# The gated layers' up products by Winograd's form of Strassen: seven half-size products for eight

## The reference

```
def swiglu_ffn(h, w1, w3, w2):
    return (jax.nn.silu(h @ w1) * (h @ w3)) @ w2

for layer in range(DEPTH_2):
    hn = rmsnorm(h, norm_mix_g[layer])
    ...
    h = h + mix
    h = h + swiglu_ffn(rmsnorm(h, norm_ffn_g[layer]), ffn_w1[layer], ffn_w3[layer], ffn_w2[layer])
return rmsnorm(h, final_g)
```

## Time and profile before

| | |
|---|---|
| median of 3 runs | 1737.45 us (1736.9 to 1738.46) |
| profiled execution: span | 1736.2 us |
| median over that span | 1.25 us more |
| TensorE, busy | 1723.5 us (99%), 8050 matmuls |
| VectorE, ScalarE, GpSimd, busy | 817.1, 688.5, 740.6 us |
| gated layer 0, from group 0's last quarter on | 738.28 to 1097.32 us |
| gated layer 1, the same | 1381.47 to 1724.2 us |

### The profile page before, as it was taken

The page is one execution under the profiler, slowest core; times in us unless marked ns, Lnnn a source line. Parts: engine busy times, 40 slices in busy tenths (PEclk is TensorE's granted clock), DMA queues, the critical chain, the costliest instruction groups (busy, mean ns, idle before and its releaser), DMA issues.

```text
span 1736.2 us, 23746 instructions
## 1 busy us (share of the span) xinstructions
PE 1723.5 (99%) x8050; PEld 1418.5 (82%) x8050; DVE 817.1 (47%) x1457; ACT 688.5 (40%) x1041; POOL 740.6 (43%) x329
## 2 busy tenths in 40 slices
PE   9999999999999999999999999999999999999998
PEld 7877778888888788888888888888888888888887
DVE  5655565333333678532332335566665523323425
ACT  5566553222222434632322224565655432322324
POOL 3232325444446297444354353442424353443441
PEclk9999999999999999999999999999999999999999
DMA  7442223322222133233233233231212332332231
GB/s 199 113 102 79 73 65 117 98 97 97 97 97 97 61 116 107 84 101 97 85 109 97 85 109 97 74 97 48 87 58 74 97 110 85 98 107 85 97 96 49
DMA packets 153686, 162.25 MB, mean 93 GB/s; under 512 B 10628, under 2 KB 114680, under 8 KB 153632
## 3 DMA queue, kind: packets, MB, share of 16 engines
q1 hardware_dynamic: 149167, 158.66, 29.7%
q10 hardware_dynamic: 4464, 2.89, 0.5%
HBM read 157.84 MB, written 3.67 MB: 93 GB/s over the span
## 4 chain that ended last, share of the span: by engine, by line
PE 95%; DVE 2%; ACT 1%; issue 0%; DMA 0%; SPq 0%; DVEq 0%; ACTq 0%
PE ps L1295 83%; PE ps L1316 2%; PE ps L1751 1%; PE ps L1643 1%; PE ps L1324 1%; PE ps L1514 1%; PE ps L1533 1%; DVE ps L2279 1%; PE ps L1426 0%; PE ps L1420 0%; PE ps L1784 0%; PE ps L1497 0%; PE ps L1430 0%; PE ps L1742 0%; PE ps L1498 0%
## 5 line engine op out<-in xcount | busy, mean ns | idle before, releaser
L640 POOL TENSOR_TENSOR wlo<-raw,whi 128x1024 fp32r<-128x1024 f32 x228 | 550.2, 2425 | 765.9 <-ACT whi L730 750.9
L1295 PE MATMUL ps<-h_hi,wlo 128*128 128x512 f32 x1376 | 546.1, 397 | 0.8 <-DVE gv L2045 0.3
L1295 PE MATMUL ps<-h_hi,whi 128*128 128x512 f32 x1376 | 536.6, 390 | 0.0
L1295 PE MATMUL ps<-h_lo,whi 128*128 128x512 f32 x1376 | 536.2, 390 | 0.0
L730 ACT ACTIVATE whi<-raw 128x1024 fp32r<-128x1024 f32 x282 | 292.7, 1055 | 503.7 <-PE ps L1295 495.1
L1295 PE MATMUL ps<-m_hi,wlo 128*128 128x512 f32 x800 | 314.5, 393 | 0.0
L1295 PE MATMUL ps<-m_hi,whi 128*128 128x512 f32 x800 | 311.5, 389 | 0.0
L1295 PE MATMUL ps<-m_lo,whi 128*128 128x512 f32 x800 | 311.4, 389 | 0.0
L1295 PEld LDWEIGHTS ps<-h_hi,whi 128*128 128x128 f32 x1376 | 258.3, 188 | 55.1
L1295 PEld LDWEIGHTS ps<-h_hi,wlo 128*128 128x128 f32 x1376 | 258.5, 188 | 54.2 <-issue 1.6
L1295 PEld LDWEIGHTS ps<-h_lo,whi 128*128 128x128 f32 x1376 | 258.6, 188 | 51.1 <-issue 0.5
(11 more groups left out here) (311 smaller groups left out, 1621.1 us busy)
## 6 DMA issues: line engine op xcount, KB each, us to landing
raw<-in_ffn_w SPq DMA_DIRECT2D x264, 256.0 KB, 2.8
raw<-in_w_ff SPq DMA_DIRECT2D x128, 256.0 KB, 2.8
raw<-in_hg_w_in SPq DMA_DIRECT2D x64, 256.0 KB, 3.1
raw<-in_w_in SPq DMA_DIRECT2D x40, 256.0 KB, 5.2
raw<-in_cp_w_in SPq DMA_DIRECT2D x24, 256.0 KB, 2.9
raw<-in_w_out SPq DMA_DIRECT2D x16, 256.0 KB, 2.9
raw<-in_cp_w_out SPq DMA_DIRECT2D x16, 256.0 KB, 2.9
raw<-in_hg_w_out SPq DMA_DIRECT2D x16, 256.0 KB, 2.9
```

The source lines that it names most:

```text
L640: pool.tensor_tensor(wlo[:, u % RING, :, :], raw[:, u % RING, :, :], whi[:, u % RING, :, :].bitcast(F32), ALU.subtract).then_inc(unit_lo, 1)
L1295: mm = pe.matmul(ps[:, b, :], wt[:, s, a, m * P:(m + 1) * P], xt[:, kts[a], :], start=starts and a == 0 and i == 0, stop=last)
```

## The change

From group 2 on, each block of an up product (w1 or w3, 256 hidden columns, all 1024 of the width, 512 tokens) is taken as a 2 x 2 product of halves (halves of the hidden columns, of the width and of the tokens) and made by seven products of 128 hidden columns, 512 of the width and 256 tokens, in place of eight. There are 18 such blocks per layer, numbered j = 0 to 17, even ones w1, odd ones w3.

- TensorE, `products(j, ...)`: per block 7 products of 4 k-tiles x 3 parts, 256 columns each. The results `y1, u2, u3, p5, c11, c12, c21` go to banks 0 to 3 in turn, so that a bank is used again three products after it is full. Down parts of two groups are put together in one `down_pair` of 96 matmuls, after every fourth block. Groups 0 and 1 are done as before. Order per layer: up 0, up 1, block 0, down pair, three turns of (blocks of four, down pair), five blocks, down pair, down of the last group.
- VectorE: four sums of quarter blocks of the weights (`weight_sum`), the low parts of forms 0, 1, 2, 3 and 5 (`low`), and the sums of the products (`add_u2` to `add_c21`), which before were two drains per block; the tokens now come normed, so `rs` is not applied there.
- GpSimd: low parts of forms 4 and 6 (`plain_low`) and of all down units, 512 columns at a time (`down_low`).
- ScalarE: the high part of each of the seven forms (`high`), a copy of `y1`, and `silu` in parts.
- Tokens: VectorE makes the normed tokens (eight tiles, `normed_tokens`), four sums of token quarters, and the low parts of seven token forms (`token_lo`, 4 x 256 columns each); ScalarE their high parts. For this the norm's sum is moved: `norm_sum` stands behind 36 of group 0's matmuls instead of 72, `sum_top` ahead of the units' splits, and three of group 0's and 1's splits behind `inv_rms`.
- Weight forms lie in 12 slots of 512 columns, eight of them the old ring. The weight transfers keep their bytes; a unit of a block has four k-tiles of 256 columns, in two transfers.

The diff, cut to its core:

```diff
+FORMS = 7
+TAGS = ("y1", "u2", "u3", "p5", "c11", "c12", "c21")
+SUM_OF = {1: 2, 2: 3, 3: 1, 5: 4}
+LOW_ON_VECTOR = (0, 1, 2, 3, 5)
+LOW_ON_GPSIMD = (4, 6)
+HALF = SEQ // 2
+SLOTS = 12
+PAIRS_IN_LOOP = 3
...
+def block_banks(j):
+    at = [(b - j) % 4 for b in (0, 1, 2, 3, 0, 1, 2)]
+    return [((tag, j), b) for tag, b in zip(TAGS, at)]
...
 # GpSimd
+                def plain_low(j, i=None):
+                    for f in LOW_ON_GPSIMD:
+                        n = block_slot(j) + f
+                        s = form_slot(layer, n)
+                        pool.wait_ge(form_hi, at(i, N_TURN, SLOTS_USED * layer + n + 1))
...
+                        pool.tensor_tensor(in_tiles(lo_slot(s)), form_source(layer, j, f),
+                                           in_tiles(hi_slot(s)).bitcast(F32), ALU.subtract).then_inc(plain_lo, 1)
...
 # ScalarE
-                def norm():
-                    sum_top(5 + 2 * layer)
-                    inv_rms(5 + 2 * layer)
-
-                up(0, 0, 0, 0, 0, norm, layer)
...
+                sum_top(5 + 2 * layer)
                 if layer == 0:
+                    split(first, 0)
+                inv_rms(5 + 2 * layer)
+                for j in range(1, 4):
+                    split(first, j)
+                for f in range(4):
+                    token_hi(f)
...
 # TensorE
+                def products(j, slots_before, i=None):
+                    for f in range(FORMS):
+                        s = form_slot(layer, block_slot(j) + f)
+                        b = part_bank(layer, j, TAGS[f])
+                        x_hi, x_lo = rounded_tokens(f)
...
+                        pe.wait_ge(drained[b], part_nth(layer, j, i, TAGS[f]) - 1)
+                        for k in range(4):
+                            for p, (wt, xt) in enumerate(((lo_slot(s), x_hi), (hi_slot(s), x_lo), (hi_slot(s), x_hi))):
+                                begins, ends = k == 0 and p == 0, k == 3 and p == 2
+                                mm = pe.matmul(ps[:, b, 0:HALF], wt[:, k * P:(k + 1) * P], xt[:, k, :],
+                                               start=begins and TAGS[f] != "c11",
+                                               stop=ends, skip_group_check=TAGS[f] == "c11")
...
-                group(first, 0, stage, up_tags, 0, 0, (0, 2, 1, 3), 0, n, norm_after(5 + 2 * layer, 2))
-                with pe.Fori(0, GLU_GROUPS // 2) as i:
-                    up(4, i * 2 + 1, i, 12)
-                    down(8, i * 2, 0, i, 12)
-                    up(10, i * 2 + 2, i, 12)
-                    down(14, i * 2 + 1, 1, i, 12)
-                down(6 * GLU_GROUPS - 2, GLU_GROUPS - 1, 0, 0, 0)
+                group(first, 0, stage, up_tags, 0, 0, (0, 2, 1, 3), 0, n, None, lambda: norm_sum(5 + 2 * layer), 1)
+                group(first, 4, stage, up_tags, 0, 0, (0, 2, 1, 3), 1)
+                products(0, 0)
+                down_pair(FORMS, 0, 0, lambda kt: pe.wait_ge(ghid_lo, 4 * layer + kt + 1))
+                with pe.Fori(0, PAIRS_IN_LOOP) as i:
+                    products(1, 2, i)
+                    for j in range(2, 5):
+                        products(j, 1, i)
+                    down_pair(N_LOOP + 4 * FORMS, 8, i + 1, parts_made(0, i), i)
+                products(TAIL, 2)
+                for j in range(TAIL + 1, TAIL + 5):
+                    products(j, 1)
...
 # VectorE
+                def normed_tokens():
+                    for k in range(KT):
+                        dve.scalar_tensor_tensor(out=n1[:, k, :] if k < 4 else ps[:, k, :], in0=xT[:, k, :],
+                                                 scalar=col("norm_ffn_g_2", KT * layer + k), in1=rs[:, :],
+                                                 op0=ALU.mult, op1=ALU.mult).then_inc(tokens_made, 1)
+                    token_step(t3[:, :, :], n2[:, :, HALF:], n1[:, :, HALF:], ALU.subtract, 8)
+                    token_step(t2[:, :, :], t3[:, :, :], n1[:, :, 0:HALF], ALU.add, 9)
+                    token_step(n1[:, :, HALF:], n1[:, :, HALF:], n1[:, :, 0:HALF], ALU.subtract, 10)
...
+                def during_up(x, y, gate_before=None, i=None):
+                    if gate_before is not None:
+                        add_c21(gate_before, i)
+                    weight_sum(y, 1, i)
+                    weight_sum(y, 2, i)
+                    low(y, 0, i)
+                    weight_sum(y, 3, i)
+                    low(y, 1, i)
+                    add_u2(x, i)
+                    low(y, 2, i)
+                    weight_sum(y, 4, i)
+                    add_u3(x, i)
+                    low(y, 3, i)
+                    add_p5(x, i)
+                    low(y, 5, i)
+                    gated_c11(x, i)
+                    add_c12(x, i)
+                    gated_c12(x, i)
...
+                dve.wait_ge(rs_ready, 6 + 2 * layer)
+                normed_tokens()
+                up_drain(0)
```

More of the change, by code:

```diff
@@ L127, in before, with glu_banks @@
         return self.nth(name, tag, turn) - 1
+def glu_banks(b, layer, up, down):
+    b.stage(f"glu{layer}", up, 2)
+    b.stage(f"glu{layer}tokens", [(("n", k), 4 + k) for k in range(4)])
+    b.stage(f"glu{layer}first", block_banks(0))
+    b.stage(f"glu{layer}loop", [x for j in range(1, 5) for x in block_banks(j)], PAIRS_IN_LOOP)
+    b.stage(f"glu{layer}tail", [x for j in range(TAIL, TAIL + 5) for x in block_banks(j)])
+    b.stage(f"glu{layer}down", down, PAIRS_IN_LOOP + 3)
 def bank_plan():
@@ L1684, in glu @@
                 first, stage = U_GLU[layer], f"glu{layer}"
-                done = 2 * GLU_GROUPS * layer
-                def up(j0, g, turn, per):
-                    group(first, j0, stage, up_tags, turn, per, (0, 2, 1, 3), g)
-                def down(j0, g, par, turn, per):
-                    for h in range(2):
-                        def tile(a):
-                            pe.wait_ge(ghid_lo, g * 2 + (done + a + 1))
-                        unit(first, j0 + h, m_hi, m_lo, (2 * par, 2 * par + 1), stage,
-                             [("d", h, m) for m in range(4)], True, True, turn, per, use=g, wait_tile=tile)
@@ new lines, in down_pair @@
+                def down_pair(n0, d0, turn, tile, i=None):
+                    for q in range(4):
+                        h, p = q // 2, q % 2
+                        s = [form_slot(layer, n0 + 2 * q + a) for a in range(2)]
+                        pe.wait_ge(down_lo, at(i, 8, DOWN_SLOTS * layer + d0 + 2 * q + 2))
+                        begun = False
+                        for a, m in [(a, m) for m in range(4) for a in range(2)] if p else [(a, m) for a in range(2) for m in range(4)]:
+                            kt = 2 * p + a
+                            if m == 0:
+                                tile(kt)
+                            if p == 0 and a == 0:
+                                pe.wait_ge(drained[4 + m], before(stage + "down", ("d", h, m), turn))
+                            for r, (wt, xt) in enumerate(((lo_slot(s[a]), m_hi), (hi_slot(s[a]), m_lo), (hi_slot(s[a]), m_hi))):
+                                last = p == 1 and a == 1 and r == 2
+                                mm = pe.matmul(ps[:, 4 + m, :], wt[:, m * P:(m + 1) * P], xt[:, kt, :],
+                                               start=kt == 0 and r == 0, stop=last)
+                                if not begun:
+                                    mm.then_inc(form_used, 2 if q else 1)
+                                    begun = True
+                                if last:
+                                    mm.then_inc(filled[4 + m], 1)
@@ L1705, in _ @@
+                for h in range(2):
+                    unit(first, LATER_UNITS + 4 + h, m_hi, m_lo, (4, 5), stage + "down", downs[h], True, True,
+                         use=PAIRS_IN_LOOP + 2, wait_tile=lambda a: made(4 + a))
             glu(0, 3)
@@ new lines, in glu @@
+                low(0, 5)
+                up_drain(1)
+                token_lo(4)
+                up_hidden(1)
+                add_u2(0)
+                token_lo(5)
+                for k in range(4):
+                    dve.sem_inc(filled[4 + k], 1)
+                add_u3(0)
+                token_lo(6)
+                up_lo(1)
+                add_p5(0)
+                dve.wait_ge(tokens_lo, FORMS * layer + 6)
+                for k in range(4):
+                    dve.sem_inc(drained[4 + k], 1)
```

610 lines of the change are left out of this document (541 added, 69 removed).

## The result

The changed kernel takes 1726.8 us (median of 4 runs, 1725.71 to 1727.73) against 1737.5 for the kernel before: ratio 0.9938, with a 95% interval of 0.9924 to 0.9952. It is faster by 10.7 us where 31 were forecast. 1726.8 lies inside the range of 1686 to 1738 and outside the forecast's own range of 1695 to 1718.

What follows compares the result with a forecast made beforehand. The prediction took TensorE, busy 99% of the span, as the bound. 1736.2 - 49.0 (short matmuls) + 12.7 (head) + 5 (VectorE in blocks) = 1704.9 us of span, median 1706; range 1686 to 1738.

Steps and rivals of the forecast that it cites:

- the forecast's own range: Whole kernel: the range of the forecast's main case, 1695 to 1718 us, given a chance of 0.50.
- The pitch of the short matmul: TensorE's blocks: a 256-column matmul takes 113.3 ns, half of 226.7, giving -49.0 us in two layers.
- the rival with the fixed excess: TensorE's blocks: 13.3 ns excess per instruction, so 120.0 ns a short matmul, kernel 1722 us; chance 0.24.
- the floor by the loads: TensorE's blocks: overlapping weight loads come no closer than 111.5 ns, giving -54 us in two layers.
- the 427 ns at 1.2 GHz: TensorE at half clock: the 512-column matmul showed no excess, taken as pointing to a stream-rate limit rather than a fixed cost.
- My own sign of being wrong: TensorE's blocks: the forecast is wrong if the pitch is over 120 ns or gaps in the blocks exceed 1 us each.
- the turn of 62.1: Loop of four blocks and a down pair: 62.1 us if the pitch is 0.120, against 59.9 us forecast.
- the estimate from the Trainium skill: TensorE's blocks: 262 cycles for 256 columns, 109.2 ns, which would give -61.5 us in two layers; not adopted.
- the rival of the exposed load: TensorE's blocks: each product waits for its whole 188 ns weight load, kernel slower at 1927 us; chance 0.05.
- VectorE in the blocks, +5: Blocks: VectorE, partly held up by GpSimd's low parts, runs late and costs 2.5 us per layer, +5 in two.
- The head, +12.7: Start of each gated layer: late first drains (4 and 4), layer 1's late norm (2.7) and slowed clock (2), +12.7 us.
- The shared inputs as a rival: Blocks: every GpSimd low part stops VectorE, prepared blocks last 10.9 and 12.1 us, kernel slower at 1749; chance 0.11.

Runs made afterwards that it cites:

- Experiment 1: A program of its own, not an edit of the kernel: streams of 96 matmuls of various widths; float32r took 120.0 ns at 256 columns, 226.7 at 512.
- experiment 7: Changed kernel with all seven low parts of a block on VectorE, none on GpSimd: 1726.8 us, ratio 0.9933.
- experiments 8 and 10: Changed kernel with block products over 192 of 256 token columns: 1715.7 us; the second also cuts GpSimd's two low parts per block to 16 columns: 1699.7 us.
- Experiment 2: Changed kernel with GpSimd's low parts of units 2 to 7 in the gated layers' head cut to 8 of 512 columns: 1712.7 us, ratio 0.9858.
- experiment 3: Changed kernel with the inverse norm also written to PSUM, where the eight normed tokens read it: 1716.8 us, ratio 0.9880.

## Why the prediction was wrong, by its steps

**The pitch of the short matmul: the step that failed.** "I take 113.3": measured 120.0 ns, the rival with the fixed excess, to which I gave 0.24. 3024 x 6.67 = 20.2 us, which is nearly all of the 20.8 by which the time was missed. I weighed the half of a known pitch and the floor by the loads against the excess, and let the 427 ns at 1.2 GHz decide. The numbers for both were there; 427 ns at half clock, with no excess, did not tell what a shorter stream does at full clock. Why there is an excess, and why none at half clock, no run here shows. My own sign of being wrong, "over 120", stood just beyond the rival's 120.0 and so could not tell the two apart; the turn of 62.1 could. Experiment 1 gives 120.0 with all other engines idle. The 109.2 ns that the estimate from the Trainium skill gave (TensorE: Matmul & The Clock Gate, Back-to-back issue gap) comes out in the same program with bfloat16 operands, 109.4 and 215.8; for float32r the measurement decides, 120.0.

**The floor by the loads: right.** 111.5 ns at 192 and 128 columns. The load was not exposed. In the last sentence on the rival of the exposed load I misread a row: the matmuls of 111.7 ns have 128 columns, whose stream is 53.3 ns and not 106.7. What it argues stands without it, since a load recorded at 188 ns doesn't fit into 111.7 unless it overlaps.

**VectorE in the blocks, +5: 0 was measured** (no wait in the loop; experiment 7 the same). The mechanism was right, as experiments 8 and 10 show: at 111.5 ns the locked low parts cost 1.8 us a turn and 16 us in all. At 120 they lie within the block's 10.08. The charge and the pitch were not independent: the fast pitch would have run into VectorE, and the rival with the fixed excess had rightly taken the charge back to +1.

**The head, +12.7: 17.5 was measured, and 0.6 elsewhere.** The kernel gained 10.7 where the pitch alone gives 28.8. Of the 18.1 the waits show 7.4 for the first drain (forecast 4 and 4), 2.6 for layer 1's norm (2.4 and 0.2 for its two matmuls; 2.7 forecast), 1.4 before block 0 and 1.0 in the first down pair (neither forecast), and the clock took 1.4 and 1.7 (2 in all forecast). Layer 0's 4.6 is to the tenth what I worked out before I rounded it down, and its terms came out too: 12.3 us for the eight tokens where the prediction had 12.5. Layer 1's came to 2.8, since the slow clock behind the norm had already made TensorE 1.7 us late there. Counted from start to start of the matmuls, against 226.7 and 120.0 ns, layer 0 loses 7.3 us and layer 1 10.2; half of the 2 us beyond the list is that each of the six gaps is 0.16 longer from start to start than the idle time shown, and the rest lies in single steps. The 0.6 us left lie outside the gated layers. Experiment 2 gets 14 of the 18 back by taking GpSimd's inputs away, experiment 3 gets 10 with the whole computation kept.

**The shared inputs as a rival** were placed wrong: they decide in the head, not in the blocks. The rule of the Trainium skill (SBUF — State Buffer, SBUF: two separate sides), by which GpSimd holds up a VectorE operation with two SBUF inputs, agrees with 3.42 and 3.10 us for operations of 1.22, and with the tokens of experiment 3, which have one and run at full pace.

**The terms add up**: the pitch was taken 20.2 us too short, the head and the rest 5.4 too short, the blocks 5 too long: 20.6 of the 20.8.

## What to carry to other kernels

This matmul, float32r with 128 stationary columns, kept its excess over the stream when it was cut from 512 columns to 256: price a shorter form with the excess in full, and run the one instruction alone when a whole change hangs on it. Where VectorE and GpSimd both read two SBUF inputs, handing work to GpSimd took almost nothing off VectorE here; one operand in PSUM freed both. Before moving an instruction forward, look at what is queued behind its wait, and on which other engine somebody waits for that; and a gap that has its cause upstream only changes its place when the instruction is moved.

## What the hardware showed that I had not expected

- Float32r with 128 stationary columns takes 112.1 ns at 240 stream columns and 119.8 at 256: 7.7 ns for 16 columns that are 6.7 at 2.4 GHz, and then 125.4 at 272, only 5.6 more for the next 16. At 448 the excess over the stream is 16 ns where 384 and 512 have 13.
- A narrower stationary operand makes the matmul faster at 256 columns (113.4 for 64) and slower at 512 (230.0 for 64, 231.7 for 32, against 226.7). No theory of mine covers both.
- GpSimd pays for the shared inputs as well: three low parts took 8.02 us beside the SBUF tokens and 7.13 beside those with an input in PSUM.
